# Attention scores as three split float32r terms, with query tiles that are stored, reloaded and split, in a hybrid RWKV7 / MLA block

## What is computed

```python
q = (rms_norm(c_q, q_norm) @ w_uq).reshape(B, S, 8, 64 + 32)      # 8 heads
q_nope, q_rope = q[..., :64], apply_rope(q[..., 64:], cos, sin)
kv = (rms_norm(c_kv, kv_norm) @ w_ukv).reshape(B, S, 8, 64 + 64)
k_nope, v = kv[..., :64], kv[..., 64:]
k_rope = apply_rope(k_rope, cos, sin)                              # one for all heads
s = (q_nope . k_nope + q_rope . k_rope) * (64 + 32) ** -0.5
s = where(key <= query, s, neg)
o = softmax(s) @ v                                                 # then o @ w_o
```

## Time and profile before

| what | value |
|---|---|
| median of 3 runs | 1555.04 us (1553.81 to 1558.23) |
| the profiled execution | 1556.18 us, span 1554.4 us |
| busy: TensorE, VectorE, ScalarE, GpSimd | 97%, 69%, 42%, 6% of the span |
| chain that ended last | TensorE 70%, VectorE 14%, DMA 9% |
| mean granted TensorE clock | 0.998 of full speed |

### The profile page before, as it was taken

How to read it: one execution, slowest core, us unless ns; L and a number is a source line. 1 busy time by engine, 2 the same in 40 slices (tenths; PEclk the granted TensorE clock), 3 DMA queues, 4 the chain that set the end, 5 groups by cost and what they waited for, 6 DMA issues and landing times.

```text
span 1554.4 us, 26228 instructions
## 1 busy us (share of the span) xinstructions
PE 1514.5 (97%) x10323; PEld 1222.9 (79%) x10323; DVE 1077.1 (69%) x1775; ACT 659.0 (42%) x1165; POOL 98.7 (6%) x178
## 2 busy tenths in 40 slices
PE   6999999999999999999999999999999999999998
PEld 6976666778787887787787887888888888788876
DVE  6468976477677491566966469777777747776786
ACT  7543454344433212444423236444444533343453
POOL 1010000000010001156100020000000000000000
PEclk9999999999999999999999999999999999999999
DMA  5030000713222535302356214444444589788754
GB/s 194 24 69 28 1 1 15 191 41 106 65 68 65 146 130 146 100 4 67 109 163 250 89 44 139 150 148 150 154 154 150 204 315 322 278 285 288 276 190 149
DMA packets 176753, 212.43 MB, mean 137 GB/s; under 512 B 28645, under 2 KB 110946, under 8 KB 176002
## 3 DMA queue, kind: packets, MB, share of 16 engines
q1 hardware_dynamic: 176574, 210.91, 40.9%
q10 hardware_dynamic: 68, 0.02, 0.0%
HBM read 154.11 MB, written 54.82 MB: 134 GB/s over the span
## 4 chain that ended last, share of the span: by engine, by line
PE 70%; DVE 14%; DMA 9%; issue 2%; SPq 2%; ACT 2%; POOL 0%; DVEq 0%; ACTq 0%; POOLq 0%
PE bank L3225 19%; PE bank L2835 13%; DMA down_raw<-in_w_ff_down 6%; PE bank L3289 5%; PE bank L3137 5%; PE bank L3190 5%; PE bank L2735 3%; PE bank L2695 2%; PE bank L2628 2%; PE bank L2748 2%; PE bank L2763 2%; DVE xprod L2048 2%; DVE mg_lo L2462 2%; DVE mg_hi L2460 1%; PE bank L2773 1%
## 5 line engine op out<-in xcount | busy, mean ns | idle before, releaser
L2835 PE MATMUL bank<-uT_hi,w_hi 128*128 128x512 f32 x432 | 171.1, 396 | 0.0
L2835 PE MATMUL bank<-uT_lo,w_hi 128*128 128x512 f32 x432 | 168.2, 389 | 0.0
L2835 PE MATMUL bank<-uT_hi,w_lo 128*128 128x512 f32 x432 | 168.2, 389 | 0.0
L3289 PE MATMUL bank<-mg_lo,mg_hi 128*128 128x512 f32 x576 | 135.3, 390 | 1.7 <-DVE mg_lo L2462 1.6
L3289 PEld LDWEIGHTS bank<-mg_lo,mg_hi 128*128 128x128 f32 x576 | 107.7, 188 | 26.2 <-DVE mg_lo L2462 3.8
L3289 PE MATMUL bank<-yh,mg_lo 128*128 128x512 f32 x384 | 118.9, 391 | 0.7 <-DVE yl L2462 0.5
L1250 ACT ACTIVATE zbuf<-bank 128x512 f32<-128x512 f32 x54 | 32.3, 598 | 186.4 <-PE bank L2835 182.4
L2835 PEld LDWEIGHTS bank<-uT_hi,w_hi 128*128 128x128 f32 x432 | 81.1, 188 | 20.7 <-issue 4.0
L1597 ACT ACTIVATE f<-f 128x512 f32<-128x512 f32 x64 | 40.4, 632 | 131.6 <-DVE f L2414 69.6
L2835 PEld LDWEIGHTS bank<-uT_hi,w_lo 128*128 128x128 f32 x432 | 81.1, 188 | 17.4 <-issue 1.0
L2835 PEld LDWEIGHTS bank<-uT_lo,w_hi 128*128 128x128 f32 x432 | 81.1, 188 | 17.0
(11 more groups left out here) (488 smaller groups left out, 3785.5 us busy)
## 6 DMA issues: line engine op xcount, KB each, us to landing
down_raw<-in_w_ff_down SPq DMA_DIRECT2D x80, 512.0 KB, 5.4
down_raw<-f_spill SPq DMA_DIRECT2D x56, 512.0 KB, 4.0
f_spill<-x SPq DMA_DIRECT2D x80, 256.0 KB, 2.7
w_raw<-in_w_in SPq DMA_DIRECT2D x28, 512.0 KB, 4.1
sgate<-gate_spill SPq DMA_DIRECT2D x16, 512.0 KB, 4.3
up_a<-in_w_ff_up SPq DMA_DIRECT2D x16, 512.0 KB, 4.7
up_b<-in_w_ff_up SPq DMA_DIRECT2D x16, 512.0 KB, 4.2
f_spill<-f SPq DMA_DIRECT2D x32, 256.0 KB, 2.3
```

The costliest lines, as they stand in the source:

```text
L2835: ins = nc.tensor.matmul(ps[2 * slot + g][:], st[:, slot, k, :], mv[:, k, g * HALF:(g + 1) * HALF], start=(k == 0 and m == 0), stop=(k == ...
L3289: ins = nc.tensor.matmul(ps[4 * (q % 2) + t][:], st, mv_, start=(start and w == 0 and m == 0), stop=(stop and w == 1 and m == 2))
```

## The change

Query and key products are split into a float32r value ("high") and its float32r rest ("low"). Of a key product, the rows of `kn` [128 rows, head, token] hold the high part on one 64-row half and the low part on the other; for tokens of half g the high part lies on rows 64g to 64g + 63. ScalarE writes the high part (two instructions of 64x512), VectorE waits for it and writes the rest (two instructions). A query product goes whole through ScalarE, scaled, into one of two staging buffers `qs` and from there to DRAM (`q_spill`); rotary query rows go to DRAM as well. SyncE reads them back by query tile: the plain rows twice, onto both halves, the rotary rows three times. ScalarE rounds them (`qh`, `qr3`), GpSimd forms the rests (`ql`, and the third copy of `qr3`). The rotary keys `kr3` stand three times: high, low, high; `qr3` high, high, low. A unit's scores are then, for each bank: `qh` (both halves) times `kn`, 128 rows; `qr3` times `kr3`, 96 rows; `ql` times the high keys, 64 rows, on the half on which they lie. The maximum is no longer multiplied by the scale. Query and key products alternate in `OUTS`. Core of the diff:

```diff
-        [...] + [(kind, g, j) for kind in ("q", "k") for j in range(NH // 2)]]
+        [...] + [(kind, g, j) for j in range(NH // 2) for kind in ("q", "k")]]
...
-                for k in range(4):
-                    g, j = k // 2, k % 2
-                    sp.wait_ge(s_rs, k + 1)
-                    for h in range(4):
-                        sp.dma_start(qT[NOPE:QH, 4 * j + h, g * HALF:(g + 1) * HALF],
-                                     qr[ROPE * h:ROPE * (h + 1), j, :]).then_inc(s_rd, 16)
+                def store_q(g):
+                    tiles = slice(4 * g, 4 * g + 4)
+                    for j in range(NH // 2):
+                        if j < 2:
+                            sp.wait_ge(s_rs, 2 * g + j + 1)
+                            sp.dma_start(qr_dram[tiles, 4 * j:4 * j + 4].rearrange("i n r q -> (n r) i q"),
+                                         qr[:, j, :].rearrange("p (i q) -> p i q", q=P)).then_inc(s_rd, 16)
+                        sp.wait_ge(s_qa, evacuated_act(OUTS.index(("q", g, j))))
+                        sp.dma_start(q_dram[tiles, :, j, :].rearrange("i p q -> p i q"),
+                                     qs[j % 2][:].rearrange("p (i q) -> p i q", q=P)).then_inc(s_qst[j % 2].sem, 16)
+                    sp.wait_ge(s_rd, 32 * (g + 1))
+                    for b in range(2):
+                        sp.wait_ge(*s_qst[b](32 * (g + 1)))
+                def load_q(i):
+                    if i >= 2:
+                        sp.wait_ge(s_sc, NH * (i - 1))
+                    for half in range(2):
+                        sp.dma_start(qn[i % 2][64 * half:64 * half + 64].rearrange("d h j q -> d h (j q)"),
+                                     q_dram[i].rearrange("(h d) j q -> d h (j q)", h=2)).then_inc(s_qt[i % 2].sem, 16)
+                def load_q_rope(i):
+                    if i >= 1:
+                        sp.wait_ge(*s_rl(i))
+                    for r in range(3):
+                        sp.dma_start(qr_in[ROPE * r:ROPE * r + ROPE, :, :], qr_dram[i].rearrange("n r q -> r n q")).then_inc(s_qrt.sem, 16)
...
+                store_q(0)
+                load_q(0)
+                load_q_rope(0)
+                load_q(1)
+                store_q(1)
                 sp.wait_ge(s_qp, OUTS.index(("q", 1, NH // 2 - 1)) + 1)
                 sp.dma_start(fw_raw[:], win[:, :, GATE0 + P:GATE0 + 2 * P]).then_inc(s_wc, 16)
+                load_q_rope(1)
+                for i in range(2, NT):
+                    load_q_rope(i)
+                    load_q(i)
+                    if i == 3:   # gate store and second fw_raw load, moved here
...
+                def q_low(i):                                    # GpSimd
+                    pool.wait_ge(*s_qh(i + 1))
+                    nc.gpsimd.tensor_tensor(ql[b][:], qn[b][:], qh[b][:].bitcast(F32), ALU.subtract).then_inc(s_ql.sem, 1)
+                    pool.wait_ge(*s_rh(i + 1))
+                    nc.gpsimd.tensor_tensor(qr3[b][r], qr_in[r], qr3[b][r].bitcast(F32), ALU.subtract).then_inc(s_rl.sem, 1)
...
+                nc.scalar.activation(kr3[2 * ROPE:3 * ROPE, :], kr3[0:ROPE, :].bitcast(F32), ACT.Copy).then_inc(s_kr, 1)
+                def q_high(i):                                   # ScalarE
+                    act.wait_ge(*s_qt[b](32 * (i // 2 + 1)))
+                    nc.scalar.activation(qh[b][:], qn[b][:], ACT.Copy).then_inc(s_qh.sem, 1)
+                def q_rope_high(i):
+                    act.wait_ge(*s_qrt(48 * (i + 1)))
+                    nc.scalar.activation(qr3[i % 2][0:3 * ROPE], qr_in[0:3 * ROPE], ACT.Copy).then_inc(s_rh.sem, 1)
...
+                        if (g, j) == (1, 1):                     # after the key product's copies
+                            q_high(0)
+                            q_rope_high(0)
+                        if (g, j) == (1, 3):
+                            q_high(1)
...
                 round_fill(0)
+                q_rope_high(1)
                 for u in range(NT * NH):
+                    if u >= NH and u // NH + 1 < NT:
+                        if u % NH == 3:
+                            q_high(u // NH + 1)
+                        if u % NH == 4:
+                            q_rope_high(u // NH + 1)
...
-                    nc.vector.tensor_scalar(small[:, 192 + u % 2:193 + u % 2], small[:, m:m + 1], SM_SCALE, None,
-                                            ALU.mult).then_inc(s_mx, 1)
...
-                    for g in range(halves(u)):
-                        w = min(n - 512 * g, 512)
-                        ins = nc.tensor.matmul(ps[b0 + g][:, 0:w], qT[0:QH, h, i * P:(i + 1) * P],
-                                               kT[0:QH, h, 512 * g:512 * g + w], start=True, stop=True)
+                    if h == 0:
+                        pe.wait_ge(*s_ql(i + 1))
+                        pe.wait_ge(*s_rl(i + 1))
+                    for o, keys, g in parts:
+                        nc.tensor.matmul(o, qh[b][:, at[0], at[1], :], kn[:, h, keys], start=True, stop=False)
+                    for o, keys, g in parts:
+                        nc.tensor.matmul(o, qr3[b][0:3 * ROPE, h, :], kr3[0:3 * ROPE, keys], start=False, stop=False)
+                    for o, keys, g in reversed(parts):
+                        r = slice(64 * g, 64 * g + 64)
+                        ins = nc.tensor.matmul(o, ql[b][r, at[0], at[1], :], kn[r, h, keys], start=False, stop=True)
```

More of the change, by code:

```diff
@@ L95 @@
 OUTS = [o for g in range(2) for o in
-        [(kind, g, j) for j in range(2) for kind in ("x", "rot")] + [(kind, g, j) for kind in ("q", "k") for j in range(NH // 2)]]
+        [(kind, g, j) for j in range(2) for kind in ("x", "rot")] + [(kind, g, j) for j in range(NH // 2) for kind in ("q", "k")]]
 OUTS += [("v", i // 4, i) for i in range(NT)]
@@ L106, in evacuated_dve @@
 def evacuated_dve(n):
-    return TABLES + sum(kind != "v" or j % 2 == 1 for kind, _, j in OUTS[:n + 1])
+    return TABLES + sum(kind != "q" and (kind != "v" or j % 2 == 1) for kind, _, j in OUTS[:n + 1])
 FILL_UNITS = 16
@@ L443, in program @@
         s_rs = sem("q_rope_summed")
-        s_rd = sem("rope_rows_spread")
+        s_rd = sem("q_rope_stored")
         s_eg = sem("early_gates_stored")
@@ L551, in program @@
         s_out = sem("out_stored")
+        s_qst = (Again(s_pos, 16), Again(s_u, 32))
+        s_qt = (Again(s_css, 16), Again(s_sin, 4))
+        s_qrt = Again(s_posf, 1)
+        s_qh, s_ql = Again(s_crt, 4), Again(s_tb, 1)
+        s_rh, s_rl = Again(s_cn, 8), Again(s_cst2, 1)
+        s_krl = Again(s_const, 2)
         s_hst = Again(s_spo, 16)
@@ L960, in _ @@
                 pool.wait_ge(s_bo, 3)
+                for i in range(1, NT):
+                    q_low(i)
                 pool.wait_ge(s_pv, NT * NH // 2)
@@ L1858, in _ @@
                 norm_c(1)
+                for g in range(2):
+                    sl = slice(g * HALF, (g + 1) * HALF)
+                    dve.wait_ge(s_kr, 2 + g)
+                    nc.vector.tensor_tensor(kr3[ROPE:2 * ROPE, sl], ps[4 + g][0:ROPE, :], kr3[0:ROPE, sl].bitcast(F32),
+                                            ALU.subtract).then_inc(s_krl.sem, 1)
                 cT_low(1)
@@ L1862, in _ @@
                     sl, bank = slice(g * HALF, (g + 1) * HALF), ps[BANKS[n % 8]]
-                    if kind == "v" and j % 2 == 0:
+                    if kind == "q" or kind == "v" and j % 2 == 0:
                         continue
@@ L1874, in _ @@
                     else:
-                        nc.vector.tensor_copy((qT if kind == "q" else kT)[0:NOPE, 2 * j + 1, sl], bank[NOPE:P, :]).then_inc(s_qd, 1)
+                        dve.wait_ge(s_qa, evacuated_act(n))
+                        for h in range(2):
+                            ins = nc.vector.tensor_tensor(kn[64 * (1 - g):64 * (1 - g) + 64, 2 * j + h, sl], bank[64 * h:64 * h + 64, :],
+                                                          kn[64 * g:64 * g + 64, 2 * j + h, sl].bitcast(F32), ALU.subtract)
+                        ins.then_inc(s_qd, 1)
                 def row_max(u):
@@ L2732, in scores @@
                         pe.wait_ge(s_ex, ex_of(u - 2) + halves(u - 2))
[L2733 to L2736 removed]
+                    b, at = i % 2, (h % 2, h // 2)
+                    if h == 0:
+                        pe.wait_ge(*s_ql(i + 1))
+                        pe.wait_ge(*s_rl(i + 1))
+                    parts = [(ps[b0 + g][:, 0:min(n - 512 * g, 512)], slice(512 * g, min(n, 512 * g + 512)), g) for g in range(halves(u))]
+                    for o, keys, g in parts:
[5 more added lines that the diff above has]
+                        ins = nc.tensor.matmul(o, ql[b][r, at[0], at[1], :], kn[r, h, keys], start=False, stop=True)
                     ins.then_inc(s_sc, 1)
```

62 lines of the change are left out of this document (41 added, 21 removed).

## The result

The changed kernel takes 1570.85 us, median of 8 runs (1563.43 to 1578.51), beside 1556.22 us for the kernel before (1553.81 to 1562.48): a ratio of 1.0094, 95% interval 1.0073 to 1.0116, slower by 0.9%. Forecast were 1557.6 us within 1546 to 1564. The profiled execution took 1563.69 us, the second fastest of the 8, with a span of 1562.0 us: 7.6 us more than before, where the medians differ by 14.6.

What follows compares the result with a forecast made beforehand. TensorE was taken to set the pace, with VectorE close behind. +3.3 us at the loop's start, +3.0 for TensorE's work and -3.7 for less waiting gave +2.6, from the median 1557.6 us, range 1546 to 1564.

Steps and rivals of the forecast that it cites:

- What bounds the kernel now: Opening step: TensorE sets the pace with VectorE close behind; no long TensorE rest, so the clock stays at 1.00.
- Cost 0: Projections, 77 to 111 us: evacuation copies stay covered by TensorE's products and eight banks; 1 to 3 us if not.
- GpSimd's subtractions: Unit loop: two subtractions per tile take 5.2 us, ready before the next tile's scores; no wait, or a short one once.
- The start: Start of unit loop: fill's weights load behind the query stores, first fill at 115.9 us, +3.3 us.
- TensorE's sum: Scores in tiles 0 to 7: shorter streams and array-shape switches nearly cancel, together +3.0 us.
- the waits: Unit loop: dropping VectorE's 0.15 us multiplication shortens TensorE's waiting for exponentials and ScalarE's copies, -3.7 us, bounds 0 and -6.4.
- The prices of the shapes: Around 64-row matmuls: entering costs 0.20 us, leaving 0.15 to 0.20, from 0.09 us gaps and exposed loads.
- the pair: Tiles 4 to 7: the two 64-row matmuls of the low-query product overlap, 0.227 us together.
- 128-column matmuls: Narrow float32r score matmuls: 0.11 us each, between half of 0.107 us for streaming alone and 0.22 us for four passes.
- slow third term: Rival, from tile 4 on: two 64-row matmuls run one after the other, +5.0 us, 1562.6 us; 0.19 together with narrow matmuls.
- late start: Rival: stores or the reload's small runs take 3 to 5 us longer, delaying the loop; 1561 to 1562 us, chance 0.09.
- Free switches: Rival, unit loop: 64-row product starts without drain or exposed load; about -11 us in the loop, 1546.5 us, chance 0.22.

Runs made afterwards that it cites:

- e5_late: Kernel before, with the load of the fill's weights waiting for the last projection instead of the last query projection; 1561.69 us, ratio 1.0036.
- e4_full: Changed kernel, with the low-query score product streaming all keys through 128 rows instead of 64; 1557.91 us, ratio 1.0021.
- e3_min: Changed kernel, with the smaller of two negated maxima taken by a one-input reduction instead of a two-input operation; 1567.26 us, ratio 1.0084.
- e1_start: Changed kernel, with the fill's weights loaded before the last query copy is stored and tile 1's rotary rows rounded at unit 3; 1567.82 us.
- e9_best: Changed kernel with earlier fill-weight load, later rotary rounding, one-input minimum, 128-row low-query product, and query tile 1's rounding moved to unit 2; 1549.95 us.
- e10_startmin: Changed kernel with earlier fill-weight load, later rotary rounding and one-input minimum, the low-query product still at 64 rows; 1559.49 us, ratio 1.0019.
- e0_after: Changed kernel measured once more without any edit, against the kernel before; 1572.86 us, ratio 1.0115.

## Why the forecast was wrong

**The clock.** The failed step is one sentence of "What bounds the kernel now": that the change takes no long rest from TensorE. The same text forecast a first fill at 115.9 us (116.3 measured) and left TensorE only the scores of two units ahead of it, a rest by its own numbers. The lateness was priced, what it does to the clock was not. Measured were rests of 1.5, 2.2 and, in tile 4, 2.3 us, 13.6 us at 1.2 GHz in the profiled loop, and clocks of 0.985 to 0.995 where the kernel before has 0.998. It is about 10 us of the 14.6 by the line through 12 runs, which gives 1560.3 us at the clock of the kernel before, inside the range; this estimate and the 7.4 us of the paragraph on GpSimd overlap, since a hold brings a fall. The rests alone don't make it all: in e5_late and e4_full TensorE rests longer ahead of the first fill (4.8 and 3.2 us), and their clocks stand at 0.995. The forecast priced the 64-row shape by its gaps and loads, and not by the clock either; without the shape the time is 1557.91 us.

**The evacuations.** "Cost 0" for the projections missed too. TensorE's products were covered by the eight banks, but VectorE's copies of the value products end 1.4 us later, and the first scores wait for them. The first exponential of the changed kernel had something later to wait for, the rotary rows; the rest that the clock's fall follows is this one.

**GpSimd's subtractions.** Their length was right (2 x 2.35 us against 5.2) and they were ready in time. But they were costed as work beside other work; that they hold an instruction of another engine was missed. It is 7.4 us in tiles 4 to 6 of the profiles, with the fall of the clock that follows. The kernel before has the same two-input instruction in each of those units (L1894), so the trace named the victim; no row of it had GpSimd at work there.

**The start.** +3.3 us with bounds +2 and +7, and the first exponential 3.5 to 5 late: measured +3.7 and +4.4. What was late next was the exponential behind the rotary rows, as said.

**TensorE's sum and the waits.** Per tile +3.3, +1.8, +1.2, +0.8, +0.8, -0.8, -1.6, -2.5 were summed. Measured, free of the held instruction (e3_min from tile 4 on) and with the short low clock of e1_start in tile 0: +3.3, +1.7, -0.3, -0.4, -0.7, -1.4, -1.7, -2.0, together -1.5. The +3.0 with the -3.7 of the waits gave -0.7. That the sums agree within 1 us is in part luck: tile 0 meets its +3.3 only with 3.4 us of low clock in it, and tiles 2 and 3 miss theirs by 1.5 and 1.2 us. The prices of the shapes held at 0.10 us a gap, the pair overlapped, and 128-column matmuls ran at one pass: at the start of e9_best's loop the matmuls of three terms begin 0.11 to 0.13 us after one another (112.16, 112.29, 112.41, 112.52 us), where a quarter of the four passes over 512 columns (two records of 0.43 us) would be 0.21.

**The rivals.** The slow third term did not come. The late start, 3 to 5 us beyond the forecast's own, did not come: the first fill was 0.4 us later than forecast and the first exponential inside its 3.5 to 5. "Free switches" did not come either; e4_full, which has no such switches, shows about 6.6 us in the tiles and not 11. None of them had the clock or a held engine, and the time on the slower side came from both.

## What to carry to other kernels

When a change makes TensorE wait for some microseconds where it did not, price the clock after the wait as well as the wait; filling the hole with work that nobody needs paid 6 to 7 us here. Look for the rest in the profile, not in the plan: the one ahead of the fall was not the one that had been expected. When work goes to GpSimd, look which VectorE instructions with two SBUF inputs run beside it, however small: a one-input form of the same step costs the same and isn't held. Splitting rows so that two matmuls overlap gains a stream and pays two changes of shape. Here the full-row matmul with the same meaning saved 2.3 us of a tile at 256 columns and cost the same at two times 512 (1.57 and 1.54 us a unit), and it kept the clock higher.

## What was not expected of the hardware

After the start of the loop the clock stayed at 1.2 GHz for 3.4, 6.8, 10.2, 17.1 or 34.1 us, with TensorE busy for 31.7 of the 34.1. The code doesn't settle the length: the changed kernel (10.2 us) and e3_min (34.1 us) have the same instructions there, and so have e1_start (3.4 us) and e10_startmin (17.1 us). The longest stretches, 17.1 and 34.1 us, were seen with the 64-row third term; without it they were 3.4 and 6.8 us in the four profiles taken, and the clocks of 79 runs (above) point the same way. Why the clock is lower with this shape, and why the length varies, stays open.

An instruction of VectorE that needs 0.16 us was held for 2.35 us where it began 7 ns after one of GpSimd (e0_after), and not at all where it began 2 ns before (the changed kernel's first profile).
